# Layer 0's last two convolved channel blocks computed as a pair of seven half products

## The reference, cut to what matters

```python
ssd_c, diff_c, mla_c = jnp.split(h_ctx @ w_in, cuts, axis=-1)
z, xbc, dt = jnp.split(p, [SSD_INNER, SSD_INNER + SSD_CONV_DIM], axis=-1)
xbc = jax.nn.silu(centred_dwconv(xbc, conv_w, conv_b))        # 768 channels, 3 taps along the tokens
xs, bm, cm = jnp.split(xbc, [SSD_INNER, SSD_INNER + SSD_GROUPS * SSD_STATE], axis=-1)
```

## Time and profile before

| | |
|---|---|
| median of three runs | 2095.87 us (2094.13 to 2097.17) |
| the profiled execution | 2094.3 us, its span 2092.2 us |
| TensorE busy | 1942.3 us (93% of the span) |
| VectorE, ScalarE, GpSimd busy | 721.6, 519.1, 186.9 us |
| memory read over the span | 508 MB |
| mean granted TensorE clock | 0.988 |

### The profile page before, as it was taken

The page is one execution under the profiler, slowest core; times in us unless marked ns, Lnnn a source line. Parts: engine busy times, 40 slices in busy tenths (PEclk is TensorE's granted clock), DMA queues, the critical chain, the costliest instruction groups (busy, mean ns, idle before and its releaser), DMA issues. The chain is left out here.

```text
span 2092.2 us, 25952 instructions
## 1 busy us (share of the span) xinstructions
PE 1942.3 (93%) x10858; PEld 934.4 (45%) x10858; DVE 721.6 (34%) x1335; ACT 519.1 (25%) x1020; POOL 186.9 (9%) x216
## 2 busy tenths in 40 slices
PE   5998999989989999999999999999898998888886
PEld 2656565544433333333334866655445333232222
DVE  2258565372431110111113476563624111111113
ACT  4146552452300000000003255524321100000012
POOL 1300000120011111212012000001100000000000
PEclk9999999999999999999999999999999999999999
DMA  9520304222289999999999223024419999999996
GB/s 351 147 81 1 141 1 152 90 105 96 82 343 401 393 399 395 394 401 393 402 395 301 111 82 141 1 90 153 165 61 357 395 408 408 408 409 409 409 409 261
DMA packets 164805, 530.64 MB, mean 254 GB/s; under 512 B 11016, under 2 KB 19538, under 8 KB 164690
## 3 DMA queue, kind: packets, MB, share of 16 engines
q1 hardware_dynamic: 149344, 489.49, 60.0%
q0 software_dynamic: 15120, 39.43, 6.1%
q10 hardware_dynamic: 226, 0.07, 0.0%
HBM read 507.98 MB, written 20.97 MB: 253 GB/s over the span
## 5 line engine op out<-in xcount | busy, mean ns | idle before, releaser
L3267 PE MATMUL ps<-ring,arena 128*64 128x512 f32 x1040 | 233.2, 597 | 13.6 <-DMA ring<-in_w_up 8.8
L3267 PE MATMUL ps<-arena 128*64 128x512 f32 x720 | 165.0, 604 | 3.6 <-DMA arena<-in_w_gate 3.2
L3267 PEld LDWEIGHTS ps<-ring,arena 128*64 128x64 f32 x1040 | 72.1, 137 | 161.6 <-issue 141.3
L3093 PE MATMUL ps<-ring,arena 128*128 128x512 f32 x320 | 141.6, 597 | 1.0 <-ACT arena L1442 0.6
L2366 DVE TENSOR_TENSOR arena<-arena,ps 128x512 f32<-128x512 f32 x32 | 22.0, 688 | 280.1 <-ACT arena L1487 280.1
L3316 PE MATMUL ps<-ring,arena 128*64 128x512 f32 x496 | 112.4, 596 | 5.8 <-DMA ring<-in_w_down 5.8
L2476 PE MATMUL ps<-arena,ring 128*128 128x256 f32 (+1 forms) x384 | 110.4, 447 | 2.5 <-DMA ring<-in_w_in 2.5
L1487 ACT ACTIVATE arena<-ps 128x512 f32<-128x512 f32 x32 | 19.1, 597 | 373.4 <-PE ps L3267 373.4
L3316 PE MATMUL ps<-arena 128*64 128x512 f32 x432 | 97.9, 595 | 5.2 <-DMA arena<-in_w_down 4.5
L1066 ACT ACTIVATE arena<-ps 128x768 f32<-128x768 f32 (+6 forms) x111 | 79.9, 724 | 88.0 <-PE ps L2494 45.3
L3267 PEld LDWEIGHTS ps<-arena 128*64 128x64 f32 x720 | 50.4, 139 | 107.0 <-issue 100.3
(11 more groups left out here) (417 smaller groups left out, 2821.8 us busy)
## 6 DMA issues: line engine op xcount, KB each, us to landing
ring<-in_w_up SPq DMA_DIRECT2D x33, 2048.0 KB, 14.7
ring<-in_w_gate SPq DMA_DIRECT2D x32, 2048.0 KB, 21.1
ring<-in_w_down SPq DMA_DIRECT2D x30, 2048.0 KB, 23.0
ring<-in_ada_w SPq DMA_DIRECT2D x24, 2048.0 KB, 9.9
arena<-in_w_down SPq DMA_DIRECT2D x19, 2048.0 KB, 23.2
arena<-in_w_gate SPq DMA_DIRECT2D x18, 2048.0 KB, 22.5
arena<-in_w_up SPq DMA_DIRECT2D x12, 2048.0 KB, 13.6
ring<-in_w_in SPq DMA_DIRECT2D x6, 2048.0 KB, 14.0
```

What stands on the lines that cost most here:

```text
L3093: ins = mm(o[:, hf * 512:(hf + 1) * 512], mix, wo[hf][:, k, :], start=k == 0, stop=k == KD - 1)
L3267: ins = mm(px[0][hf * 64:hf * 64 + 64, col:col + 512], xl[e % 2][:, at:at + CAP_L], w[c][:, hf * 512:hf * 512 + 512], start=b + c == 0, st ...
```

## The change

In layer 0 only, blocks 4 and 5 become a third pair: seven half products of 384 tokens, with four sums of weights on VectorE (`bc_weight_sums`), seven sums of products (`bc_halves`) and one copy on ScalarE. The results go to `CM[4]` and `CM[5]`, which are the memory of `CM[0]` and `CM[2]`. Layer 0's order of blocks becomes 2, 0, 3, 1, 5, 4. The first of the seven products is issued ahead of `block_rows(l, 2, 2)`, the other six behind it. Layer 1 keeps the old code with new counts. The core of the diff (first the tables, then ScalarE's loop over the blocks, VectorE's new functions and its loop, and TensorE's new order):

```diff
+        CM += [CM[0], CM[2]]
-        CONV_ORDER = (2, 0, 3, 1, 4, 5)
+        CONV_ORDER = ((2, 0, 3, 1, 5, 4), (2, 0, 3, 1, 4, 5))
+        def last_pair_of_channels(x):
+            return SW[1 + x // 2][:, :, P * (x % 2):P * (x % 2) + P]
...
+                    if l == 0 and m == 1:
+                        act.wait_ge(S["half_products"], products0 + 11)
+                        act.activation(E1[0], J.tile(conv_job(l, 4))[:, 0:HT], ACT.Copy).then_inc(S["half_out"], 1)
...
+                def bc_weight_sums():
+                    dve.wait_ge(*J.filled(conv_job(l, 2)))
+                    half_sum(s_[0], wb15[:, 0:4, P:2 * P], wb15[:, 4:8, P:2 * P], ALU.add)
+                    sums_done(21)
+                    half_sum(s_[1], s_[0], wb15[:, 0:4, 0:P], ALU.subtract)
+                    sums_done(22)
+                    half_sum(s_[2], wb15[:, 0:4, 0:P], wb15[:, 0:4, P:2 * P], ALU.subtract)
+                    half_sum(s_[3], wb15[:, 4:8, 0:P], s_[1], ALU.subtract)
+                def bc_halves():
+                    dve.wait_ge(S["half_out"], out0 + 3)
+                    dve.wait_ge(S["half_products"], products0 + 12)
+                    half_sum(CM[4][:, 0:HT], E1[0], J.tile(j0)[:, 0:HT], ALU.add)
+                    dve.wait_ge(S["half_products"], products0 + 13)
+                    half_sum(E1[0], E1[0], J.tile(j0)[:, 512:512 + HT], ALU.add)
+                    sums_done(28)
+                    dve.wait_ge(*J.filled(j0))
+                    TT(U3[0], E1[0], J.tile(j0)[:, 512:512 + HT], ALU.add).then_inc(*J.free(j0))
+                    dve.wait_ge(*J.freed(j0))
+                    half_sum(CM[5][:, HT:TOK], U3[0], J.tile(j1)[:, 0:HT], ALU.add)
+                    half_sum(E1[0], E1[0], J.tile(j1)[:, 0:HT], ALU.add)
+                    dve.wait_ge(S["half_products"], products0 + 15)
+                    half_sum(CM[5][:, 0:HT], U3[0], J.tile(j1)[:, 512:512 + HT], ALU.add)
+                    sums_done(30)
+                    dve.wait_ge(*J.filled(j1))
+                    TT(CM[4][:, HT:TOK], E1[0], J.tile(j1)[:, 0:HT], ALU.add).then_inc(*J.free(j1))
...
-                for m in CONV_ORDER:
+                for m in CONV_ORDER[l]:
                     if m == 3:
                         early_half(1)
+                        if l == 0:
+                            bc_weight_sums()
                         last_half(1)
+                    if m == 5 and l == 0:
+                        bc_halves()
...
+                else:
+                    pe.wait_ge(*J.empty(conv_job(l, 4)))
+                    bc_product(0, 0, w[:, 0:4, 0:P], rows_half(0, 0)).then_inc(S["half_products"], 1)
+                    block_rows(l, 2, 2)
+                    pe.wait_ge(S["half_out"], out0 + 3)
+                    bc_product(0, 0, w[:, 4:8, 0:P], rows_half(4, 0)).then_inc(S["half_products"], 1)
+                    pe.wait_ge(S["half_sums"], sums0 + 24)
+                    bc_product(0, 1, last_pair_of_channels(1), TH[1]).then_inc(S["half_products"], 1)
+                    pe.wait_ge(*J.empty(conv_job(l, 5)))
+                    bc_product(1, 0, last_pair_of_channels(0), TH[0]).then_inc(S["half_products"], 1)
+                    pe.wait_ge(S["half_sums"], sums0 + 28)
+                    bc_product(0, 1, last_pair_of_channels(2), TH[2]).then_inc(*J.fill(conv_job(l, 4)))
+                    bc_product(1, 1, w[:, 4:8, P:2 * P], TH[3]).then_inc(S["half_products"], 1)
+                    pe.wait_ge(S["half_sums"], sums0 + 30)
+                    bc_product(1, 0, last_pair_of_channels(3), rows_half(4, 1)).then_inc(*J.fill(conv_job(l, 5)))
```

More of the change, by code:

```diff
@@ L609, in build, with plain @@
         assert h0 + 4 * HT + TOK <= h1 - 704
-        CONV_ORDER = (2, 0, 3, 1, 4, 5)
+        CM += [CM[0], CM[2]]
+        CONV_ORDER = ((2, 0, 3, 1, 5, 4), (2, 0, 3, 1, 4, 5))
+        def last_pair_of_channels(x):
+            return SW[1 + x // 2][:, :, P * (x % 2):P * (x % 2) + P]
+        def plain(l, m):
+            return l > 0 and m >= 4
         XC = 640 + SG
@@ L1300, in _ @@
                     act.wait_ge(s_xst, 16 * nq)
-                products0, sums0 = 10 * l, 22 * l
+                products0, sums0 = 15 * l, 33 * l
                 for p in range(2):
@@ L1312, in _ @@
                 act.activation(dts[1], dts[1], ACT.Ln).then_inc(S["dt_log"], 1)
-                for i, m in enumerate(CONV_ORDER):
+                for i, m in enumerate(CONV_ORDER[l]):
                     j = conv_job(l, m)
-                    if m in (2, 3):
+                    if plain(l, m):
+                        act.wait_ge(*J.filled(j))
+                    elif m in (2, 3):
                         act.wait_ge(S["half_sums"], sums0 + (15, 20)[m - 2])
-                    elif m < 2:
-                        act.wait_ge(*J.freed(conv_job(l, 2 * m + 1)))
+                    elif m == 5:
+                        act.wait_ge(S["half_sums"], sums0 + 31)
                     else:
-                        act.wait_ge(*J.filled(j))
+                        act.wait_ge(*J.freed(conv_job(l, 5 if m == 4 else 2 * m + 1)))
                     on = slice(conv_start(l, m), TOK)
-                    src = CM[m] if m < 4 else J.tile(j)
+                    src = J.tile(j) if plain(l, m) else CM[m]
                     act.activation(XB[:, m, on], src[:, on], ACT.Identity, bias=pc[:, R_CB + m:R_CB + m + 1],
                                    scale=pc[:, R_CW + CONV_T + m:R_CW + CONV_T + m + 1]).then_inc(S["conv_mid"], 1)
-                    if m < 4:
-                        act.wait_ge(S["half_sums"], sums0 + (16, 19, 21, 22)[i])
+                    if l == 0 and m == 1:
+                        act.wait_ge(S["half_products"], products0 + 11)
+                        act.activation(E1[0], J.tile(conv_job(l, 4))[:, 0:HT], ACT.Copy).then_inc(S["half_out"], 1)
+                    if not plain(l, m):
+                        act.wait_ge(S["half_sums"], sums0 + (16, 19, 25, 26, 32, 33)[i] - (0 if l == 0 or i < 2 else 4))
                     else:
@@ L1865, in _ @@
                     dve.wait_ge(s_xst, 16 * nq)
-                sums0, out0, products0 = 22 * l, 2 * l, 10 * l
+                sums0, out0, products0 = 33 * l, 3 * l, 15 * l
                 n10 = block_base(l) + 10
@@ L1973, in _ @@
                 last_half(0)
-                for m in CONV_ORDER:
+                def bc_weight_sums():
+                    n15 = block_base(l) + 15
+                    dve.wait_ge(ring_full[n15 % RING], ring_turns(n15) * 16)
+                    wb15, s_ = ringv(n15), [last_pair_of_channels(x) for x in range(4)]
+                    dve.wait_ge(*J.filled(conv_job(l, 2)))
[6 more added lines that the diff above has]
+                def bc_halves():
+                    j0, j1 = conv_job(l, 4), conv_job(l, 5)
+                    dve.wait_ge(S["half_out"], out0 + 3)
[15 more added lines that the diff above has]
+                for m in CONV_ORDER[l]:
                     j = conv_job(l, m)
@@ L1979, in _ @@
                         early_half(1)
+                        if l == 0:
+                            bc_weight_sums()
                         last_half(1)
+                    if m == 5 and l == 0:
+                        bc_halves()
                     dve.wait_ge(*v.next(S["conv_mid"]))
-                    src, dst = CM[m] if m < 4 else J.tile(j), XB[:, m, :]
+                    src, dst = J.tile(j) if plain(l, m) else CM[m], XB[:, m, :]
                     for tap, sh in ((0, -1), (2, 1)):
@@ L2850, in _ @@
                 w = arrived(wb + 10)
-                sums0, out0 = 22 * l, 2 * l
+                sums0, out0 = 33 * l, 3 * l
                 def weight(p, half, k0):
@@ L2891, in _, with bc_product @@
                 w = arrived(wb + 15)
-                feature_major(conv_job(l, 4), w, 0, P)
-                block_rows(l, 2, 2)
-                feature_major(conv_job(l, 5), w, P, P, conv_start(l, 5) // P)
+                if l:
+                    feature_major(conv_job(l, 4), w, 0, P)
+                    block_rows(l, 2, 2)
+                    feature_major(conv_job(l, 5), w, P, P, conv_start(l, 5) // P)
+                else:
+                    def bc_product(i, hf, a, b):
+                        o = J.tile(conv_job(l, 4 + i))[:, 512 * hf:512 * hf + HT]
+                        for k in range(4):
+                            ins = mm(o, a[:, k, :], b[:, k, :], start=k == 0, stop=k == 3)
+                        return ins
+                    pe.wait_ge(*J.empty(conv_job(l, 4)))
+                    bc_product(0, 0, w[:, 0:4, 0:P], rows_half(0, 0)).then_inc(S["half_products"], 1)
+                    block_rows(l, 2, 2)
+                    pe.wait_ge(S["half_out"], out0 + 3)
[9 more added lines that the diff above has]
+                    bc_product(1, 0, last_pair_of_channels(3), rows_half(4, 1)).then_inc(*J.fill(conv_job(l, 5)))
                 pe.wait_ge(*w_.next(S["la_ready"]))
```

## The result

| | before | changed |
|---|---|---|
| median (lowest to highest, runs) | 2095.60 us (2094.13 to 2097.17, 4) | 2110.57 us (2108.14 to 2114.12, 4) |
| profiled execution, its span | 2094.3, 2092.2 us | 2108.14, 2106.1 us |

The ratio is 1.0073, its 95% interval 1.0054 to 1.0091: slower by 15.0 us in the medians, 13.9 in the spans of the two profiled executions, against 11.4 forecast.

A forecast was written before the change was run, and what follows sets the result against it. The prediction took TensorE to bound the kernel: -2.8 (products) + 5.4 (load wait) + 5.4 (ps1 wait) + 3.4 (clock) = +11.4 us, giving 2107.3 us against the median of 2095.87; range 2101.5 to 2111.5.

The forecast's parts named there:

- What bounds: Layer 0's projection and expert stage: TensorE sets the pace, 200.00 of 200 us busy in the latter; its delay moves the end.
- rival 3: Expert stage runs at the pace of its loads, so TensorE catches up: 2095.9 us, or 2093; chance 0.03.
- The products: Blocks 4 and 5 on TensorE: seven half products, 18.06 us, replace 20.83 us, removing 2.8 us.
- The load of block 14: Before block 14's modulation rows: the load lands at 351.9, so TensorE waits 5.4 us from 346.49.
- What hides: Behind the wait for block 14's load: weight sums (2.75 us) and ScalarE's copy, done by 351.6, cost nothing.
- The slot ps1 for `acT`: Before `acT`: ps1 is held until VectorE adds modulation rows at 377.1, wanted at 371.7; a 5.4 us wait.
- The clock: TensorE's clock falls after each of two new waits, 2 x 1.7 = 3.4 us; bounds per wait 0 and 3.4.
- The sum: Whole kernel: 8.0 us at full clock plus 3.4 for the clock, +11.4 us, forecast 2107.3 us.
- rival 2: Clock stays low for the long stretch after one or both new waits: up to +14.8 us, 2110.7; chance 0.12.
- rival 1: Both new waits appear but TensorE's clock stays up: +8.0 us, 2103.9; chance 0.14.

The follow-up runs named there:

- The kernel with everything mended: mended order, plus VectorE's copies of the cumulated sums and third set of rows moved between block 5's and block 4's taps; 2095.05 us, ratio 0.9994.
- the run with the rows added early: Changed kernel with VectorE's step that frees ps1 for `acT` moved from behind block 4's taps to behind the new pair's second sum; 2108.12 us, ratio 1.0069.
- the fillers: Changed kernel with unread matmuls in its two idle times, eleven before the modulation rows and eight before `acT`; 2105.00 us, ratio 1.0047.
- mended order: Changed kernel with block 14's modulation rows behind the fourth product, ScalarE's copy behind block 3's middle tap, and ps1 freed early; 2102.28 us, ratio 1.0029.
- the copy late: As mended order, but with ScalarE's copy left behind block 1's middle tap; 2103.58 us, ratio 1.0043.
- the gate's wait filled: As mended order, with four unread matmuls in TensorE's wait before the gate; 2098.03 us, ratio 1.0013.

## Why the prediction was right, and where it was off

- **What bounds.** Right. TensorE's delay in the projection reached the end whole (13.30 there, 13.92 at the last group), and the expert stage gave nothing back: rival 3 falls.
- **The products.** Right: with 2.77 us for them the split closes to 0.01. The kernel with everything mended shows 1.73 of it beside a hole of 0.58.
- **The load of block 14.** The number was right (351.9; the runs have 352.1 and 351.9), but not the step built on it, "the modulation rows behind it wait for `ring_full2` until 351.9". The same instruction also waits for `ps_free1`, as its row in the order shows. Two sets of modulation rows take ps1 one after the other, and VectorE frees the first one behind block 1's taps. This term of the sum was 5.4 and measured 7.5. That it missed by only 2.1 is luck: the slot came free 1.9 us behind the load, and nothing in the prediction kept it from coming later.
- **What hides.** I followed the four sums of weights to the copy on ScalarE, found it covered, and costed them at nothing. They push everything behind them on VectorE, so also the step that frees ps1, by 1.7 us, and that one was not covered. The copy was, exactly as I said: it ended at 351.4, forecast 351.6.
- **The slot ps1 for `acT`.** Right: forecast 377.1 - 371.7 = 5.4, measured 380.70 - 375.30 = 5.40, the whole shifted by the first term. What I did not see is that the next two steps were close behind: the run with the rows added early met the gate's slot, 3.0 us.
- **The clock.** Right in kind: it fell behind both holes, and filling them kept it up. Forecast 2 x 1.7 = 3.4, measured 3.1, 3.2 and 4.7 in three traces. By wait they are 1.46, 1.68, 1.48, 1.70, 2.50 and 2.24, all between the bounds of 0 and 3.4. That the forecast price fits two of the three traces is in part luck: I took a stretch of 3.4 us wholly behind each wait, and at the first one the stretch was longer and began inside it. The Trainium skill, "TensorE: Matmul & The Clock Gate", "What's actually happening", calls the half rate the default that activity lifts; the fillers agree with that (sixteen records in 1.92 us behind them, 3.28 without). The profiled run of the change lies at the low end of its runs, which is why the medians differ by 15.0 and the spans of the profiled executions by 13.9.
- **The sum.** 8.0 + 2.1 for the missed slot + 3.1 for the clock = 13.2, against 13.30 in the trace. The measured median, 2110.57, is nearly the number of rival 2 (2110.7), but not by its mechanism: that took 3.4 us lost behind each wait, and no trace shows more than 2.50. The trace has the missed slot instead, and the rest of the medians' 15.0 lies in executions without a trace.

## What to carry to other kernels

When a product is split so that the cheaper form starts with a short piece, the filler behind that piece loses its cover: list everything that the filler's first instruction waits for, loads and slots alike, and take the latest of them, with every release moved by what was put in front of it on its own engine. Look at loops whose side steps are tied to one index (`if m in (1, 4)`): reversing two indices moved a step that frees a slot from the middle of the loop to its end. And count the fall of TensorE's clock as part of a wait's price; where a wait cannot be removed, useless matmuls in it can pay.

## What had not been expected of the hardware

The length of a short wait does not decide what clock TensorE gets behind it. A wait of 2.98 us before the gate was followed by a low clock in one trace (mended order, 11.37 us for the gate) and not in another (rows added early, 8.22 us), nor was one of 2.97 us with the copy late (8.22). The ten runs of the mended order fell into two groups whose middles, 2099.5 and 2105.6, are 6.1 us apart.

The same is seen near 42 us, ahead of everything that the change or an experiment touches. In ten of the twelve traces the clock fell there, behind 2.23 to 2.65 us of idle time: behind 2.45 us in the kernel before (granted clock 0.66), and behind 2.33 us with the order mended (0.66). In two it did not: behind 2.64 us with both holes filled, and behind 2.53 us with the gate's wait filled. Their rows for 42 to 47 us both have a granted clock of 1.00, the first of them being:

```profile
42.00:47.00 5.00, 5.00 (x13) 2.25 (x12) 2.74 (x11) 1.83 (x5) 2.39 (x4) 1.00 1.03 376
```

Those two traces start block 4 at 342.00 and 342.18 us, where the others have 343.44 to 343.92. So the reading behind the prediction's rival 1, that 2.33 us leave the clock alone and 2.45 us do not, was one draw of several.

A wait of 1.88 us in the scan, the same in both, left the clock alone in the kernel before and did not with the order mended (windows around it, before and mended, granted clock 1.00 and 0.91):

```profile
425.00:445.00 20.00, 18.10 (x101) 9.38 (x102) 16.91 (x26) 9.16 (x21) 5.97 (x6) 1.00 0.00 1
```

```profile
430.00:450.00 20.00, 18.11 (x96) 9.21 (x94) 17.00 (x26) 8.63 (x20) 5.79 (x5) 0.91 0.00 1
```

So what short waits cost differs between executions by some us in stages that an edit doesn't touch. Whether the shift of a few us from the edit has a part in it, as in the scan, was not tried: near 42 us it happened without one.
